# Moving the attention norm's scale per token from the operand of the query, key and value projections to their results

## The chip, the cores and the metric

The kernel runs on one core of one Trainium2 chip. The metric is the device time of one execution in microseconds (us). Three executions of the kernel before gave 984.69, 985.72 and 985.86 us.

## The reference

Two transformer blocks run one after the other on 256 tokens of width 1024, all in 32-bit floats. The change concerns the seam between them: the first block ends in a modulated norm, and the second begins with an attention norm and the query, key and value projections.

```python
def first_block(...):
    ...
    shf, scf = jnp.split(c_act @ w_ada_f + b_ada_f, 2, axis=-1)
    return modulate(rms_norm(x, normf_w), shf, scf)

def second_block(x, attn_norm, w_qkv, ...):
    h = x
    y = rms_norm_2(h, attn_norm[i])
    qkv = (y @ w_qkv[i]).reshape(B, S, 3, N_HEADS, HEAD_DIM)
    ...
    o = moba_attention(q, k, v, rel_bias)
    h = h + o.transpose(0, 2, 1, 3).reshape(B, S, D) @ w_o[i]
```

`rms_norm` divides each token by the root of its mean square (plus 1e-6) and multiplies by a weight per feature; `modulate` is h * (1 + scale) + shift with a scale and a shift per feature. With 256 tokens the attention is plain causal attention of 16 heads of width 64 with a bias by distance. Its scores are divided by 8 and go through a softmax.

## The kernel before

Activations are stored transposed: 128 features on the partitions, 256 tokens along the free dimension, eight such tiles for width 1024. `X` is the residual stream. A token's scale is then a value per column, which the kernel holds in `R`, the same in all partitions: the squares of `X` are summed over features by matmuls with a matrix of ones, and ScalarE takes logarithm and exponential of the sum (`act_ln_exp`, L1315 and L1317).

**Products.** Every large product is made of three passes in a reduced format (float32r). The operand is split into a high part `HH` and a low part `HL`, the weight into `wh` and `wl`, and the matmul engine adds wh*HH, wl*HH (L997) and wh*HL (L1003). A unit is four 128-row slices of a weight by 256 output columns; it is done as two tiles of twelve matmuls, one for each 128 outputs, and a projection product has two units, so four tiles. Value products swap the operands, so tokens lie on the partitions of their result (L995 and L1001). ScalarE rounds a unit's weight to `wh` (L1330), VectorE subtracts to get `wl` (L1682), in five buffers in turn: the split of the unit four ahead waits until the unit before the running one is done with its buffer.

**The seam.** The last product of the first feed-forward network ends in `close`: VectorE adds it to `X` (L1743), ScalarE squares, the matmul engine sums, then does two sets of nine small warming matmuls (L1112), and ScalarE makes `R`. Then `after` writes the modulated `X` in place: VectorE multiplies by weight and scale (`shift`, L1752), ScalarE adds the shift (L1384). ScalarE and VectorE square these tiles by turns (L1356, L1715), the matmul engine sums them (L1159, L1160), ScalarE makes the second `R`, and `apply` makes the operands: VectorE multiplies `X` by the attention norm's weight and `R` into `tmp` (`dve_scale`, L1644), ScalarE rounds to `HH` (L1305), VectorE and GpSimd subtract to `HL` (L1657, L1901). Only then can the first query product start. The feed-forward norm of the first block uses the same `apply` with a shift: there ScalarE makes the odd tiles in two steps (L1307, L1309) and the even ones in one (L1311).

**Attention.** Products come in the order q0, k0, q1, k1, v0, q2, k2, v1, q3, k3, v2, v3, each with 256 outputs, that is four heads. ScalarE evacuates each result from its accumulation bank (`act_evacuate`: L1234 for queries, with the factor 1/8, L1236 for keys, L1238 for values). Four heads at a time go through `attend`: scores on the matmul engine (L1094, L1095), bias and maximum on VectorE (L1567, L1569), exponentials on ScalarE (L1282, L1284), division on VectorE (L1577, L1578), transposes on the matmul engine (L1100), and the product with the values (L1106, L1107).

**What sets the order.** A planner written in Python (`run`, `after`, `tick`) puts out one list of events. Each engine walks it and takes its own part, so each engine's order is fixed when the kernel is built, and engines wait for one another on semaphores. Tasks such as `attend` are generators that `tick` advances by a step after each tile of a product.

## Time and profile before

| | us |
|---|---|
| three executions, median | 985.72 |
| the profiled execution | 986.15 |
| its span on the core | 984.4 |
| matmul engine busy | 939.0 |
| VectorE busy | 677.4 |
| ScalarE busy | 505.7 |
| GpSimd busy | 75.3 |
| DMA, mean rate | 180 GB/s |

The span is cut by time: the mixer of the first block comes first, its feed-forward network ends near 647, the seam lies from there to 663, the projections and the attention to about 758, and the second feed-forward network fills the rest. Busy times are sums over the span; what counts for the time is which engine the others wait for. A timeline lists an engine's instructions by start in microseconds from the span's start, with the idle time before one and what released it. The granted clock is TensorE's, 1.00 for its full 2.4 GHz and 0.50 for 1.2 GHz.

### The profile page before, as it was taken

The numbers are of one execution on the slowest core, as the hardware profiler recorded it, in microseconds if no ns is written. First come the engines' busy times: TensorE is split into PE (matmuls) and PEld (weight loads), VectorE is DVE, ScalarE is ACT, GpSimd is POOL, SyncE is SP. The second block draws the span as 40 slices with busy tenths as digits, with TensorE's granted clock in tenths as the row PEclk, the third lists the DMA queues.
The fourth block names the chain that finished last, engine by engine and source line by source line (L and its number), as shares of the span: only waits on it lengthen the run. The fifth ranks groups of instructions, "written<-read, shape, count | busy, mean of one in ns | idle before, by whom it ended". The sixth has DMA issues, their size and how long they took to land.

```text
span 984.4 us, 17542 instructions
## 1 busy us (share of the span) xinstructions
PE 939.0 (95%) x7500; PEld 898.9 (91%) x7500; DVE 677.4 (69%) x1102; ACT 505.7 (51%) x805; POOL 75.3 (8%) x91
## 2 busy tenths in 40 slices
PE   6789999999999999999998999989999999999997
PEld 2588998998999999999998999979998999999997
DVE  3877678567569888678677774556665677777643
ACT  2476666544343456556334443456665465666442
POOL 0101112112100000021000000110000300000001
PEclk9799999999999999999999999999999999999999
DMA  8733222222248977455899775514442354554631
GB/s 321 281 144 120 87 87 86 87 91 87 82 166 299 337 288 273 154 201 212 243 271 338 270 279 182 202 46 172 134 156 97 129 172 174 187 197 161 219 135 43
DMA packets 27677, 177.41 MB, mean 180 GB/s; under 512 B 2864, under 2 KB 5680, under 8 KB 7504
## 3 DMA queue, kind: packets, MB, share of 16 engines
q1 hardware_dynamic: 27600, 176.30, 51.2%
q8 instruction: 59, 0.97, 0.4%
q14 instruction: 18, 0.15, 0.1%
HBM read 174.45 MB, written 1.84 MB: 179 GB/s over the span
## 4 chain that ended last, share of the span: by engine, by line
PE 71%; DVE 13%; DMA 7%; ACT 7%; issue 2%; SPq 0%; DVEq 0%; ACTq 0%
PE ps L997 37%; PE ps L1003 19%; DVE wl L1682 3%; DMA raw<-in_w_fi_dram 3%; DVE acc L1617 2%; ACT wh L1330 2%; PE ps L1050 2%; PE ps L995 2%; PE ps L1039 2%; DMA raw<-in_w_sc_dram 1%; DMA raw<-in_w_rest_dram 1%; DVE tmp L1644 1%; PE ps L1046 1%; DMA raw<-in_w_in_dram 1%; PE ps L1132 1%
## 5 line engine op out<-in xcount | busy, mean ns | idle before, releaser
L997 PE MATMUL ps<-HH,wh 128*128 128x256 f32 x1480 | 386.1, 293 | 7.0 <-DVE wl L1682 6.1
L1682 DVE TENSOR_TENSOR wl<-raw,wh 128x1024 fp32r<-128x1024 f32 x265 | 321.8, 1235 | 99.5 <-ACT wh L1330 98.9
L997 PE MATMUL ps<-HH,wl 128*128 128x256 f32 x1480 | 374.4, 285 | 0.0
L1330 ACT ACTIVATE wh<-raw 128x1024 fp32r<-128x1024 f32 x265 | 272.3, 1040 | 175.5 <-PE ps L1003 105.3
L997 PEld LDWEIGHTS ps<-HH,wh 128*128 128x128 f32 x1480 | 286.2, 193 | 13.8 <-issue 8.6
L997 PEld LDWEIGHTS ps<-HH,wl 128*128 128x128 f32 x1480 | 286.3, 193 | 2.0 <-issue 2.0
L1003 PE MATMUL ps<-HL,wh 128*128 128x256 f32 x1480 | 241.2, 285 | 2.6 <-DVE HL L1657 2.2
L1003 PEld LDWEIGHTS ps<-HL,wh 128*128 128x128 f32 x1480 | 207.1, 194 | 3.4 <-DVE HL L1657 2.6
L997 PE MATMUL ps<-FH,wl 128*128 128x256 f32 x352 | 88.8, 285 | 0.0
L997 PE MATMUL ps<-FH,wh 128*128 128x256 f32 x352 | 88.1, 279 | 0.0
L1617 DVE SCALAR_TENSOR_TENSOR acc<-raw,silc,acc 128x512 f32<-128x512 f32 x101 | 76.6, 759 | 8.7 <-DMA raw<-in_ada_dram 5.7
L997 PEld LDWEIGHTS ps<-FH,wh 128*128 128x128 f32 x352 | 66.9, 190 | 0.0
L1600 DVE SCALAR_TENSOR_TENSOR tmp<-ps,vec,tmp 128x255 f32<-128x255 f32 (+2 forms) x112 | 46.1, 475 | 29.5 <-ACT tmp L1400 27.8
L997 PEld LDWEIGHTS ps<-FH,wl 128*128 128x128 f32 x352 | 66.0, 187 | 0.0
L1003 PE MATMUL ps<-FL,wh 128*128 128x256 f32 x352 | 57.8, 282 | 0.0
L1906 POOL TENSOR_TENSOR sq<-sq 128x256 f32<-128x256 f32 x12 | 10.7, 888 | 600.2 <-ACT sq L1368 600.2
L1003 PEld LDWEIGHTS ps<-FL,wh 128*128 128x128 f32 x352 | 48.9, 188 | 0.0
L1534 DVE TENSOR_TENSOR xz<-xz,ps 128x512 f32<-128x512 f32 x32 | 21.8, 687 | 32.1 <-PE ps L1050 32.1
L1491 ACT ACTIVATE FH<-tmp 128x512 fp32r<-128x512 f32 x22 | 13.9, 633 | 58.0 <-DVE tmp L1846 30.4
L997 PE MATMUL ps<-YH,wh 128*128 128x256 f32 x128 | 32.2, 281 | 1.4 <-DVE wl L1682 1.4
L997 PE MATMUL ps<-YH,wl 128*128 128x256 f32 x128 | 32.1, 284 | 0.0
L1400 ACT ACTIVATE tmp<-ps,vec 128x256 f32<-128x256 f32 x44 | 22.3, 556 | 14.7 <-PE ps L1003 14.7
(251 smaller groups left out, 1148.1 us busy)
## 6 DMA issues: line engine op xcount, KB each, us to landing
raw<-in_ada_dram SPq DMA_DIRECT2D x32, 1024.0 KB, 5.2
raw<-in_w_fi_dram SPq DMA_DIRECT2D x22, 1024.0 KB, 5.0
raw<-in_w_up_dram SPq DMA_DIRECT2D x22, 1024.0 KB, 4.8
raw<-in_w_rest_dram SPq DMA_DIRECT2D x20, 1024.0 KB, 4.9
raw<-in_w_in_dram SPq DMA_DIRECT2D x16, 1024.0 KB, 4.8
raw<-in_w_qkv_dram SPq DMA_DIRECT2D x12, 1024.0 KB, 4.8
raw<-in_w_o_dram SPq DMA_DIRECT2D x8, 1024.0 KB, 4.9
raw<-in_w_fo_dram SPq DMA_DIRECT2D x8, 1024.0 KB, 5.1
```

What stands on the lines that cost most here:

```text
L995: e.matmul(o, x_hi[:, k0 + k, 128 * t:128 * t + 128], w[:, k, :], start=first and n + k == 0, **MM)
L997: e.matmul(o, w[:, k, 128 * t:128 * t + 128], x_hi[:, k0 + k, :], start=first and n + k == 0, **MM)
L1003: ins = e.matmul(o, wh[:, k, 128 * t:128 * t + 128], x_lo[:, k0 + k, :], start=False, **MM)
L1039: ins = e.matmul(bank[:, cs[c]], S[f"d{n % 2}"][:, c, :], xz[:, 0, c, :], start=True, **MM)
L1050: ins = e.matmul(bank[:, 256 + 128 * c:384 + 128 * c], S["y"][:, c, :], xz[:, 1, c, :], start=True, **MM)
L1330: e.activation(whl[u % HALF][0][:, 0:n], raw[i % RAW][:, c:c + n], ACT.Copy).then_inc(*a_hi.up(u))
L1400: e.activation(tmps[m][:, T * t:T * t + T], b[:, T * t:T * t + T], ACT.Identity, scale=v("conv2", 88 + ft), bias=v("conv2_b", ft)).then_in ...
L1491: e.activation(flat(dst, j), tmps[m][:, :], ACT.Copy).then_inc(*a_ev.up("hi", src, j))
L1534: e.tensor_tensor(xz4, xz4, b[:, :], ALU.subtract).then_inc(*v_gdn.up("xz", h, n))
L1600: e.scalar_tensor_tensor(out=cv, in0=b[:, T * t:T * t + T - s], scalar=tap, in1=cv, op0=ALU.mult, op1=ALU.add).then_inc(*v_ev.up("conv", n ...
L1617: ins = e.scalar_tensor_tensor(out=acc_, in0=w, scalar=c, in1=acc_, op0=ALU.mult, op1=ALU.add)
L1682: e.tensor_tensor(wl[:, 0:n], raw[i % RAW][:, c:c + n], wh[:, 0:n].bitcast(F32), ALU.subtract).then_inc(*v_lo.up(u))
```

## The change

The scale of the attention norm is a factor per token, so it can be left out of the operand and multiplied into the result. The operand becomes X * w1n * R + shn, where `R` is now the scale of the first block's last norm, `w1n` its weight times the attention norm's and `shn` the modulation's shift times the attention norm's weight. `apply(N3)` makes it straight from `X` before `X` is modulated, with the instructions of the feed-forward norm. The modulation of `X`, its squares, their sums and the second scale move into a task, `third_norm`, which runs beside the first query product; its scale is kept in `R3`, an eighth of it in `R3q`, and, turned by two matmuls of one column, per partition in `r3c`. Queries and keys are evacuated by VectorE with a multiplication by `R3q` or `R3`, values by ScalarE in two halves with `r3c`. The vectors `w1c`, `w1n` and `shn` are made ahead of the closing residual. The second set of warming matmuls goes.

```diff
+    w1n = sb("w1n", [128, 8])
+    shn = sb("shn", [128, 8])
...
+    R3 = sb("R3", [128, T], where=phase)
+    R3q = sb("R3q", [128, T], where=phase)
+    r3c = sb("r3c", [128, 2], where=phase)
...
+    def third_norm():
+
+        bank, before = yield from take(misc)
+        for i in range(4):
+            emit("shift", N2, i)
+            s, sfree = yield from take(sq)
+            yield
+            emit("norm_sq", N3, i, s, sfree, bank, before if i == 0 else None)
+            sq.give(s, p_norm, "sq", N3, i)
+        yield
+        emit("norm_r", N3, bank)
+        made.add("norm_r3")
+        misc.give(bank, a_norm, "ln", N3)
+        yield
+        bank, before = yield from take(misc)
+        emit("norm_col", N3, bank, before)
+        made.add("norm_col")
+        misc.give(bank, a_norm, "col")
+        misc.order[:] = [b for b in misc.order if b[0] == 3]
...
         elif kind in ("q2", "k2", "v2"):
-            emit("plain", p["p"], 0)
-            main.give(banks[0], a_ev, "plain", p["p"])
+            until("norm_r3" if kind != "v2" else "norm_col")
+            if kind == "v2":
+                emit("plain", p["p"], 0)
+                main.give(banks[0], a_ev, "plain", p["p"])
+            else:
+                emit("normed", p["p"], 0)
+                main.give(banks[0], v_ev, "normed", p["p"])
...
+            if n == N1:
+                mod(4)
+                mod(3)
+                emit("mod_scale", n, 0)
+            elif n == N2:
+                mod(7)
+                mod(6)
+                emit("mod_scale", n, 0)
             close(n, p)
             for t in range(2):
                 main.give(banks[t], v_ev, "x", n, 6 + t)
             if n == N1:
-                mod(4)
-                mod(3)
-                emit("mod_scale", n, 0)
                 apply(n)
             elif n == N2:
-                mod(7)
-                mod(6)
-                emit("mod_scale", n, 0)
-                bank, before = misc.take()
-                for i in range(4):
-                    emit("shift", n, i)
-                    if i:
-                        s, sfree = sq.take()
-                        emit("norm_sq", N3, i - 1, s, sfree, bank, before if i == 1 else None)
-                        sq.give(s, p_norm, "sq", N3, i - 1)
-                s, sfree = sq.take()
-                emit("norm_sq", N3, 3, s, sfree, bank, None)
-                sq.give(s, p_norm, "sq", N3, 3)
-                wbank, wfree = misc.take()
-                emit("norm_r", N3, bank, wbank, wfree)
-                misc.give(wbank, p_norm, "warm", N3)
-                misc.give(bank, a_norm, "ln", N3)
                 apply(N3)
-                misc.order[:] = [b for b in misc.order if b[0] == 3]
+                tasks.append(third_norm())
...
-            a_ev.wait_ge(e, "plain", named["q2", j]["p"])
-            a_ev.wait_ge(e, "plain", named["k2", j]["p"])
+            v_ev.wait_ge(e, "normed", named["q2", j]["p"])
+            v_ev.wait_ge(e, "normed", named["k2", j]["p"])
...
-            elif kind == "norm_r" and ev[1] == N3:
-                warm(e, N3, *ev[3:])
+            elif kind == "norm_col":
+                b = ev[2]
+                free(e, ev[3])
+                a_norm.wait_ge(e, "r", N3)
+                for t in range(2):
+                    ins = e.matmul(psum[b][:, t:t + 1], R3[0:1, cs[t]], ones[0:1, 0:1], start=True, **MM)
+                ins.then_inc(*p_norm.up("col"))
...
-        elif kind == "q2":
-            ins = e.activation(flat(QA, j), bank[:, :], ACT.Copy, scale=0.125)
-        elif kind == "k2":
-            ins = e.activation(flat(KA, j), bank[:, :], ACT.Copy, scale=1.0)
         else:
-            ins = e.activation(VA[:, :, 256 * j:256 * j + 256], pair(bank), ACT.Copy)
+            a_norm.wait_ge(e, "col")
+            e.activation(VA[:, 0, 256 * j:256 * j + 256], bank[:, 0:T], ACT.Copy, scale=r3c[:, 0:1]).then_inc(
+                *a_ev.up("plain_0", n))
+            ins = e.activation(VA[:, 1, 256 * j:256 * j + 256], bank[:, T:2 * T], ACT.Copy, scale=r3c[:, 1:2])
...
+                act_ln_exp(e, n, b)
                 if n == N3:
-                    v_norm.wait_ge(e, "shift", 7)
-                act_ln_exp(e, n, b)
+                    a_norm.wait_ge(e, "r", N3)
+                    e.activation(R3q[:, :], R3[:, :], ACT.Copy, scale=0.125).then_inc(*a_norm.up("rq"))
+            elif kind == "norm_col":
+                p_norm.wait_ge(e, "col")
+                e.activation(r3c[:, :], psum[ev[2]][:, 0:2], ACT.Copy).then_inc(*a_norm.up("col"))
...
+            x_ready(e, N2 if n == N3 else n, kt)
+            w = {N3: w1n[:, kt:kt + 1], N4: v("ffn_norm", kt)}.get(n, w1c[:, kt:kt + 1])
...
+        if n == N2:
+            mod_ready(e, 12, 13)
+            e.tensor_tensor(shn[:, :], modc[:, 48:56], v("attn_norm", 0, 8), ALU.mult).then_inc(*v_norm.up("shn"))
+            v_norm.wait_ge(e, "w1c", N2, 0)
+            e.tensor_tensor(w1n[:, :], w1c[:, :], v("attn_norm", 0, 8), ALU.mult).then_inc(*v_norm.up("w1n"))
...
+            elif kind == "normed":
+                p = products[ev[1]]
+                finished(e, p)
+                a_norm.wait_ge(e, "rq" if p["kind"] == "q2" else "r", *(() if p["kind"] == "q2" else (N3,)))
+                dst, r = (QA, R3q) if p["kind"] == "q2" else (KA, R3)
+                e.tensor_tensor(dst[:, 2 * p["j"]:2 * p["j"] + 2, :], pair(psum[p["banks"][0]]),
+                                r[:, None, :].broadcast_to([128, 2, T]), ALU.mult).then_inc(
+                    *v_ev.up("normed", ev[1]))
```

The matmul engine's order at the seam before (`ps` are banks, `sq` squares, `cst` the ones and the identity, `wh0` and `wl0` the first unit's weight):

```order
L1112 MATMUL ps4<-cst 128x128 x9
L1159 MATMUL ps4<-sq2,cst 128x256
L1160 MATMUL ps4<-sq2,cst 128x256
L1159 MATMUL ps4<-sq0,cst 128x256
L1160 MATMUL ps4<-sq0,cst 128x256
L1159 MATMUL ps4<-sq1,cst 128x256
L1160 MATMUL ps4<-sq1,cst 128x256
L1159 MATMUL ps4<-sq2,cst 128x256
L1160 MATMUL ps4<-sq2,cst 128x256
L1112 MATMUL ps3<-cst 128x128 x9
L997 MATMUL ps2<-HH,wh0 128x256
```

And now, from the warming matmuls on; between the last rows of a pair and the next pair stands one tile:

```order
L1130 MATMUL ps4<-cst 128x128 x9
L1015 MATMUL ps2<-HH,wh0 128x256
...
L1021 MATMUL ps2<-HL,wh0 128x256 x4
L1177 MATMUL ps4<-sq2,cst 128x256
L1178 MATMUL ps4<-sq2,cst 128x256
L1015 MATMUL ps2<-HH,wh0 128x256
...
L1177 MATMUL ps4<-sq2,cst 128x256
L1178 MATMUL ps4<-sq2,cst 128x256
L1184 MATMUL ps3<-cst,R3 128x1 x2
L1015 MATMUL ps0<-HH,wh2 128x256
```

The four pairs of ones matmuls moved from ahead of the query product to behind each of its four tiles, and the two one-column matmuls stand between the last pair and the key product.

ScalarE's order at the seam before, from the shifts of `X` to the weight splits:

```order
L1384 ACTIVATE X<-X,modc 128x256 x4
L1356 ACTIVATE sq2<-X 128x512
L1384 ACTIVATE X<-X,modc 128x256 x4
L1356 ACTIVATE sq1<-X 128x512
L1315 ACTIVATE R<-ps4,cst 128x256
L1317 ACTIVATE R<-R 128x256
L1305 ACTIVATE HH<-tmp3 128x256 x2
L1305 ACTIVATE HH<-tmp0 128x256 x2
L1305 ACTIVATE HH<-tmp1 128x256 x2
L1305 ACTIVATE HH<-tmp2 128x256 x2
L1330 ACTIVATE wh4<-raw0 128x1024
```

And now, from the last rounding to `HH` on:

```order
L1333 ACTIVATE HH<-tmp2 128x256
L1413 ACTIVATE X<-X,modc 128x256 x2
L1355 ACTIVATE wh4<-raw0 128x1024
L1381 ACTIVATE sq2<-X 128x512
L1413 ACTIVATE X<-X,modc 128x256 x4
L1355 ACTIVATE wh0<-raw0 128x1024
L1381 ACTIVATE sq1<-X 128x512
L1413 ACTIVATE X<-X,modc 128x256 x2
L1340 ACTIVATE R3<-ps4,cst 128x256
L1342 ACTIVATE R3<-R3 128x256
L1388 ACTIVATE R3q<-R3 128x256
L1391 ACTIVATE r3c<-ps3 128x2
```

Shifts, squares and the second logarithm and exponential moved behind the roundings, with two weight splits (`wh4`, `wh0`) between them.

VectorE's order ahead of the second group of heads before (`OLl` is the output of the group before, `ISA` the bias and maximum):

```order
L1581 TENSOR_TENSOR OLl<-ps6,OHh 64x256
L1581 TENSOR_TENSOR OLl<-ps7,OHh 64x256
L1567 ISA ap0,ast0<-ps4,U 128x128
L1567 ISA ast0 128x1
L1569 ISA ap0,ast0<-ps4,U 128x256
L1569 ISA ast0 128x1
L1572 TENSOR_SCALAR ast0<-ast0 128x2
```

And now:

```order
L1610 TENSOR_TENSOR OLl<-ps6,OHh 64x256
L1610 TENSOR_TENSOR OLl<-ps7,OHh 64x256
L1838 TENSOR_TENSOR QA<-ps1,R3q 128x512
L1596 ISA ap0,ast0<-ps4,U 128x128
L1596 ISA ast0 128x1
L1598 ISA ap0,ast0<-ps4,U 128x256
L1598 ISA ast0 128x1
L1601 TENSOR_SCALAR ast0<-ast0 128x2
```

The evacuation of the query product moved from ScalarE to this place, ahead of the first head's bias and maximum; the third group of heads has the same rows.

## Rows read from the trace of the kernel before

**Rows 1.** The page, the chain that ended last, share of the span by engine.
```profile
PE 71%; DVE 13%; DMA 7%; ACT 7%; issue 2%; SPq 0%; DVEq 0%; ACTq 0%
```

**Rows 2.** Waits of the matmul engine, 640 to 790: us in all, times, longest.
```profile
PE ps L1100 <- DVE ap L1578: 2.1, 6, 0.4
```

**Rows 3.** Timeline of VectorE around the norm: start us, us, instructions [idle before <-releaser].
```profile
645.93 0.48 DVE L1743 SCALAR_TENSOR_TENSOR X<-ps,modc,X 128x256 f32<-128x256 f32 x1 [1.22 <-PE ps L1003]
...
647.05 0.16 DVE L1667 SCALAR_TENSOR_TENSOR w1c<-modc,vec 128x8 f32<-128x8 f32 x1
649.33 2.46 DVE L1752 SCALAR_TENSOR_TENSOR X<-X,w1c,R 128x256 f32<-128x256 f32 x6 [2.12 <-ACT R L1317]
...
658.59 1.67 DVE L1644 SCALAR_TENSOR_TENSOR tmp<-X,vec,R 128x256 f32<-128x256 f32 x4 [4.03 <-ACT R L1317]
```

**Rows 4.** The same of ScalarE.
```profile
649.85 1.71 ACT L1384 ACTIVATE X<-X,modc 128x256 f32<-128x256 f32 x4 [0.55 <-DVE X L1752]
651.47 0.61 ACT L1356 ACTIVATE sq<-X 128x512 f32<-128x512 f32 x1
```

**Rows 5.** The same of the matmul engine.
```profile
652.22 0.67 PE L1159 MATMUL ps<-sq,cst 128*128 128x256 f32 x2 [1.88 <-ACT sq L1356]
...
654.13 1.06 PE L1160 MATMUL ps<-sq,cst 128*128 128x256 f32 x2
654.98 1.06 PE L1159 MATMUL ps<-sq,cst 128*128 128x256 f32 x2
...
657.44 2.17 PE L1112 MATMUL ps<-cst 128*128 128x128 f32 x18
...
663.08 0.28 PE L997 MATMUL ps<-HH,wh 128*128 128x256 f32 x1
...
667.38 0.28 PE L997 MATMUL ps<-HH,wh 128*128 128x256 f32 x1
```

**Rows 6.** Timeline, feed-forward norm: VectorE twice, ScalarE, matmul engine.
```profile
444.61 1.68 DVE L1644 SCALAR_TENSOR_TENSOR tmp<-X,w1c,R 128x256 f32<-128x256 f32 x4 [2.14 <-ACT R L1317]
...
450.85 0.48 DVE L1614 TENSOR_SCALAR acc<-raw,silc 128x512 f32<-128x512 f32 x1
...
451.04 1.99 ACT L1330 ACTIVATE wh<-raw 128x1024 fp32r<-128x1024 f32 x2
...
449.26 0.27 PE L997 MATMUL ps<-HH,wh 128*128 128x256 f32 x1
```

**Rows 7.** Stretches: us, busy (instructions) by engine, granted clock, DMA share, GB/s.
```profile
653.10:656.30 3.20, 3.20 (x10) 2.45 (x9) 0.78 (x2) 1.16 (x3) 0.00 (x0) 0.50 0.02 5
...
752.50:755.30 2.80, 1.64 (x9) 0.93 (x9) 2.32 (x11) 2.80 (x11) 0.00 (x0) 1.00 0.81 334
755.50:758.50 3.00, 3.00 (x16) 2.19 (x18) 1.26 (x2) 2.17 (x7) 0.00 (x0) 0.50 0.01 3
```

**Rows 8.** Timeline of VectorE, first group of heads.
```profile
675.01 0.29 DVE L1567 CUSTOM_DVE_ANT_0 ap<-ps,U 128x128 f32<-128x128 f32 x1 [2.23 <-PE ps L1095]
...
679.54 0.35 DVE L1578 TENSOR_SCALAR ap<-ap,ast 128x256 f32<-128x256 f32 x1
...
681.51 0.35 DVE L1578 TENSOR_SCALAR ap<-ap,ast 128x256 f32<-128x256 f32 x1
```

**Rows 9.** Timeline, second group of heads: VectorE, ScalarE, matmul engine twice.
```profile
701.38 0.29 DVE L1567 CUSTOM_DVE_ANT_0 ap<-ps,U 128x128 f32<-128x128 f32 x1 [2.35 <-PE ps L1095]
...
703.77 0.60 ACT L1234 ACTIVATE QA<-ps 128x512 f32<-128x512 f32 x1 [3.62 <-PE ps L1003]
...
707.89 1.44 PE L1100 MATMUL ps<-cst,ap 128*128 128x128 f32 x9
709.67 0.55 PE L1100 MATMUL ps<-cst,ap 128*128 128x128 f32 x3 [0.33 <-DVE ap L1578]
```

**Rows 10.** Groups by shape: busy us, mean ns | idle before <-releasers.
```profile
L1846 DVE TENSOR_TENSOR tmp<-tmp,ps 128x512 f32<-128x512 f32 x11 | 7.5, 685 | 6.3 <-PE ps L1003 6.3
...
L1406 ACT ACTIVATE tmp<-ps,vec 128x256 f32<-128x256 f32 x8 | 3.4, 470 | 8.1 <-PE ps L1003 8.1
```

More of the change, by code:

```diff
@@ L1300, in act_parts @@
                 finished(e, named[before_write[n]])
-            shift = {N0: modc[:, kt:kt + 1], N1: modc[:, 24 + kt:25 + kt]}.get(n)
+            shift = {N0: modc[:, kt:kt + 1], N1: modc[:, 24 + kt:25 + kt], N3: shn[:, kt:kt + 1]}.get(n)
+            if n == N3:
+                v_norm.wait_ge(e, "shn")
             if n in (N0, N1):
@@ L1313, in act_ln_exp @@
     def act_ln_exp(e, n, b):
+        r = R3 if n == N3 else R
         ln_exp(e)
-        e.activation(R[:, :], psum[b][:, 0:T], ACT.Ln, scale=1.0 / 1024, bias=eps).then_inc(*a_norm.up("ln", n))
+        e.activation(r[:, :], psum[b][:, 0:T], ACT.Ln, scale=1.0 / 1024, bias=eps).then_inc(*a_norm.up("ln", n))
         a_norm.wait_ge(e, "ln", n)
-        e.activation(R[:, :], R[:, :], ACT.Exp, scale=-0.5).then_inc(*a_norm.up("r", n))
+        e.activation(r[:, :], r[:, :], ACT.Exp, scale=-0.5).then_inc(*a_norm.up("r", n))
     def scalar_engine(e):
@@ L1636, in dve_scale @@
     def dve_scale(e, n, j, m, before):
-        a_norm.wait_ge(e, "r", n)
+        a_norm.wait_ge(e, "r", N2 if n == N3 else n)
         if n in (N0, N1):
             v_norm.wait_ge(e, "w1c", n, j // 2 if n == N0 else 0)
+        if n == N3:
+            v_norm.wait_ge(e, "w1n")
         free(e, before)
         for kt in (2 * j, 2 * j + 1):
-            x_ready(e, n, kt)
-            w = {N3: "attn_norm", N4: "ffn_norm"}.get(n)
-            e.scalar_tensor_tensor(out=tmps[m][:, T * (kt % 2):T * (kt % 2) + T], in0=X[:, kt, :],
-                                   scalar=w1c[:, kt:kt + 1] if w is None else v(w, kt), in1=R[:, :], op0=ALU.mult,
-                                   op1=ALU.mult).then_inc(*v_norm.up("scaled", n, kt))
+            x_ready(e, N2 if n == N3 else n, kt)
+            w = {N3: w1n[:, kt:kt + 1], N4: v("ffn_norm", kt)}.get(n, w1c[:, kt:kt + 1])
+            e.scalar_tensor_tensor(out=tmps[m][:, T * (kt % 2):T * (kt % 2) + T], in0=X[:, kt, :], scalar=w,
+                                   in1=R[:, :], op0=ALU.mult, op1=ALU.mult).then_inc(*v_norm.up("scaled", n, kt))
     def dve_parts(e, n, j, m):
@@ L1651, in dve_parts @@
         src, high = tmps[m][:, 0:T], HH[:, kt, :].bitcast(F32)
-        if n in (N0, N1):
-            shift = modc[:, kt:kt + 1] if n == N0 else modc[:, 24 + kt:25 + kt]
+        if n in (N0, N1, N3):
+            shift = {N0: modc[:, kt:kt + 1], N1: modc[:, 24 + kt:25 + kt], N3: shn[:, kt:kt + 1]}[n]
             ins = e.scalar_tensor_tensor(out=HL[:, kt, :], in0=src, scalar=shift, in1=high, op0=ALU.add,
```

## The prediction

> **What bounds the kernel now.** I read the page first. The chain that ended last lies on the matmul engine for 71% of the span [rows 1], so a step pays where it takes a wait away from that engine, and costs where it puts one there. Next come the matmul engine's waits in the stretch that the change rebuilds: the attention transposes wait 2.1 us in six pieces [rows 2]. The timelines of three engines then show the norm itself. VectorE gets the scale of the first block's last norm at 649.33 [rows 3]. ScalarE's shift of a tile follows VectorE's by 0.52 us, four shifts take 1.71 us and a 128x512 square 0.61 us [rows 4]. The matmul engine waits 1.88 us for the first squares, starts the sums at 652.22 and ends them at 657.44; 1.15 us later VectorE has the second scale [rows 3, 5]. It reaches tile 2 of the query product (a tile is twelve matmuls, four per product) at 663.08 and the key product at 667.38, so three tiles take 4.30 us, 1.43 each [rows 5]. That is the stage to beat: from 649.33 to 667.38, 18.05 us.
>
> Inside it the clock matters. After 1.88 us without work the sums run at half: the granted clock is 0.50 from 653.1 to 656.3 (the lower level, 1.2 GHz, where 1.00 is 2.4 GHz) [rows 7]; I put its return at 656.5, 4.3 us after work resumed at 652.22 [rows 5]. At the lower level a ones matmul takes 0.85 us (654.13 to 654.98) [rows 5], at the full one half of that, so a pair costs 1.70 or 0.85.
>
> **The change, part by part.** Times t count from 649.33, when VectorE has the first scale in either kernel.
>
> *Operands without the second norm.* Scaling, shifting and splitting has a model in the feed-forward norm, which has the same instructions and starts at 444.61: tile 1 ends there at 449.26, VectorE is free at 450.85, ScalarE at 451.04 [rows 6]. So tile 1 ends at t = 4.65, VectorE is free at 6.24, ScalarE at 6.43. Before, tile 1 ended at t = 13.75. The matmul engine is 9.1 us ahead here.
>
> *The norm beside the product.* In the new order a pair of ones matmuls stands behind each of the four tiles. Each engine works in order, so tile 2 can't start before the first squares. VectorE starts the first two tiles of the residual stream at 6.24 and 6.64 (six took 2.46 us [rows 3]); ScalarE shifts them from 6.76 to 7.6, then has a weight split to do (1.99 us for two [rows 6], so 0.95), and squares at 8.55 to 9.16. The pair starts 0.14 later, at 9.3: **4.65 us idle**, more than twice the idle time that was followed by the half clock. I therefore take the lower level from 9.3 on, and 4.3 us of it, as before: pair 1 to 11.0, tile 2 to 13.7. ScalarE's next split waits for tile 2 (its buffer), 13.8 to 14.8; it squares to 15.4, shifts the last two tiles to 16.15, and VectorE squares them to 16.9. The matmul engine meanwhile: pair 2 to 14.6 (0.85 again), tile 3 to 16.0, pair 3 to 16.9, tile 4 to 18.3, pair 4 to 19.2. Logarithm and exponential with their hand-overs take the 1.15 us seen at 657.44, to 20.35, and the two one-column matmuls, which wait for them, about 0.4: the key product starts at t = 20.75 where it did at 18.05. **+2.7 us.** At the full level all along the same steps give pair 1 to 10.15, tile 2 to 11.6, squares and pair 4 to 17.1, the key product at 18.6: +0.55. These are the ends of the range for this term. I take the first, since an idle stretch less than half as long was enough.
>
> *Key evacuation on VectorE.* The nearest row is a 128x512 multiply out of PSUM, 685 ns [rows 10], against 0.60 us on ScalarE [rows 9]: +0.1 us ahead of the first scores. The weight split now behind it delays VectorE by as little.
>
> *Query evacuation ahead of the scores.* For query products 2 and 3 VectorE's order is now: evacuate the query product, then add bias and find the maxima of four heads. The product is only finished one tile behind those heads' score matmuls. Before, ScalarE evacuated it at 703.77, while VectorE had begun on the scores at 701.38 and their last transposes started at 709.67, 0.33 us after the ones before [rows 9]. Now VectorE waits until 703.77, evacuates for 0.61 (685 ns less the 0.08 by which neighbours overlap) and begins on the scores at 704.38. From there to the last normalized tile the first group of heads needs 6.85 us (675.01 to 681.51 + 0.35) [rows 8]: 711.23. The last transposes follow at once, **1.6 us** later than the 709.67 of before, and the matmul engine has nothing else, since the next tile stands behind them. ScalarE saves its 0.6 us of evacuation, but no longer sets the pace. Bounds: nothing, if ScalarE still did, to 3.0 us, the whole delay at the start. The working lies between and I keep it: twice, **+3.2 us**. Later splits slip by 3 us and are made three products' units ahead, so they cover it.
>
> *Value evacuation in two.* Two scaled copies (470 ns each [rows 10], the second some 0.05 earlier than end to end) take 0.87 instead of 0.60 us. Three of the four stand ahead of no exponentials; the last heads the chain of waits to the last heads' exponentials: **+0.25 us**.
>
> *Small ones.* The scale vectors made ahead of the closing residuals: one takes 0.16 us, and at the attention norm VectorE was idle 1.22 us ahead of them, which hides all three [rows 3]; at the feed-forward norm I grant no such cover, +0.1 us. The copy of the scale for queries costs ScalarE 0.4 us while the key product runs: nothing. The nine warming matmuls that go were inside a wait.
>
> Sum: 2.7 + 0.1 + 3.2 + 0.25 + 0.1 = 6.35 us on the profiled execution's 986.15. That run is 0.43 above the median of 985.72; on the median I say **992.1 us**.
>
> **A rule against a row.** From 752.5 to 755.3 the matmul engine was busy 1.64 of 2.80 us at the full clock, with no wait over 0.4 us, and yet the clock was at half from 755.5 to 758.5 [rows 2, 7]. The new stalls in the two middle groups of heads look alike: twelve transposes spread over 3.7 us, first gap 1.3 us (they began at 707.89 [rows 9]; the heads' last steps on VectorE come 0.66 us apart [rows 8] and end at 711.23, so the first tile is there at 709.25). The Trainium skill, TensorE: Matmul & The Clock Gate, section "Why this matters for your kernels", blames idle gaps between bursts of matmuls, and asks that none be long. By that rule the transposes would keep the full clock and the sum stands; by the row it may fall there too, which is rival 1. The trace agrees with the rule at 653 and goes beyond it at 755.
>
> **The rivals.**
> 1. *The clock falls in the middle groups too.* For: the row just named. Against: in those groups before, transposes with single gaps of 0.33 us did not bring it. A stretch of 3.0 to 3.2 us at the half level [rows 7] costs up to 1.6 us where the engine has work: 993.7 with one, 995.3 with both.
> 2. *The clock holds beside the first product.* Then 2.7 becomes 0.55: 989.9. Against it stands the stretch at 653.1 [rows 7].
> 3. *The norm is hidden after all* (the other side). If each square is ready when its pair is reached, the matmul engine goes through: 4.65 + four pairs 3.5 + three tiles 4.3 + 1.5 for the scale = t 13.95, which is 4.1 us earlier than before. With the other terms, 3.65, the time is 985.3, not slower. It decides at the first pair: the squares would have to be ready by t = 4.65, while VectorE is bound to splitting operands until 6.24. If only the later pairs are in time, the 4.65 us of idle time stand and nothing is won.
> 4. *The stalls in the middle groups are absorbed*: the working gives a wait of 1.6 us, its lower bound none. Without them 988.9.
>
> **How the numbers follow.** Forecast 0.42; rival 1 0.30 (two groups, each about one in five); rival 2 0.13; rival 4 0.08; rival 3 0.05; something else 0.02. The range takes the forecast, rivals 1 and 2: low 989.0 is just under rival 2, high 995.6 just above rival 1 with both groups. A measurement of this kernel can tell about 0.2%, 2.0 us, from no change. Slower by more than that (over 987.7) are all cases but rival 3 and part of the rest: 0.93. Rival 3 lies within 0.2%: 0.04 of it there, and 0.03 for faster in all, where the clock also happens to hold where it fell before.
>
> **What the new profile would show.** The first tile of the query product ends near t = 4.65, then the matmul engine waits some 4.6 us for a square of ScalarE, at half clock afterwards; the key product starts 20 to 21 us behind the first scale. A wait of about 1 us stands ahead of the one-column matmuls. In the two middle groups VectorE idles until the query product's last matmul, and transposes wait for VectorE some 1.3 us at first. Wrong would be: a wait under 2 us ahead of the first pair, a key product earlier than t = 18, or transposes that still end ScalarE's chain.

## The result and the profile after

| | median us | executions | ratio to the kernel before | 95% interval |
|---|---|---|---|---|
| kernel before | 985.3 | 20 | | |
| changed kernel | 989.6 | 20 | 1.0045 | 1.0032 to 1.0059 |

The change costs 4.4 us (3.2 to 5.8, the ratio's interval times 985.3). The forecast was 992.1, with 989.0 to 995.6 as its range.

The profiled execution of the changed kernel took 984.37 us, the lowest of its twenty, so its end says nothing; distances inside it do. The stage begins again where VectorE has the first scale, here at 642.78 (t = 0), where [rows 3] has 649.33. First the chain that ended last and the matmul engine's waits, 640 to 790:

```profile
PE 80%; DVE 10%; ACT 5%; DMA 3%; issue 1%; SPq 0%; DVEq 0%; ACTq 0%
```

```profile
PE ps L1177 <- ACT sq L1381: 4.9, 1, 4.9
PE ps L1118 <- DVE ap L1607: 4.3, 6, 1.2
...
PE ps L1184 <- ACT R L1342: 1.0, 1, 1.0
```

The 1.9 us ahead of the first ones matmuls [rows 5] have become 4.9, and the transposes' 2.1 [rows 2] have become 4.3; a wait of 1.0 for the scale is new. The timelines of the matmul engine, VectorE and ScalarE at the seam show how:

```profile
652.53 1.19 PE L1177 MATMUL ps<-sq,cst 128*128 128x256 f32 x2 [4.94 <-ACT sq L1381]
...
663.63 0.60 PE L1184 MATMUL ps<-cst,R 1*128 1x1 f32 x4 [1.01 <-ACT R L1342]
671.05 0.50 PE L1112 MATMUL ps<-KA,QA 64*128 64x128 f32 x4 [0.87 <-DVE KA L1838]
```

```profile
642.78 1.67 DVE L1675 SCALAR_TENSOR_TENSOR tmp<-X,w1n,R 128x256 f32<-128x256 f32 x4 [2.19 <-ACT R L1342]
...
649.02 1.36 DVE L1787 SCALAR_TENSOR_TENSOR X<-X,w1c,R 128x256 f32<-128x256 f32 x2
```

```profile
650.41 0.51 ACT L1413 ACTIVATE X<-X,modc 128x256 f32<-128x256 f32 x1 [0.38 <-DVE X L1787]
...
651.77 0.61 ACT L1381 ACTIVATE sq<-X 128x512 f32<-128x512 f32 x1
```

VectorE starts the residual stream at t = 6.24, as forecast; ScalarE shifts two tiles, splits a weight and squares at 8.99; the first sums start at 9.75 (forecast 9.3). The first scores start at t = 28.27, where they started at 24.75 before. And in this execution the granted clock falls inside the wait already, at t = 7.48, and is back at t = 14.31 (the columns of [rows 7]):

```profile
647.00:650.00 3.00, 0.51 (x2) 0.30 (x2) 3.00 (x7) 2.06 (x5) 1.42 (x2) 1.00 0.00 0
650.00:652.00 2.00, 0.00 (x0) 0.00 (x0) 2.00 (x4) 1.62 (x4) 0.10 (x1) 0.56 0.00 0
652.00:655.00 3.00, 2.47 (x7) 2.14 (x8) 1.99 (x5) 1.75 (x5) 0.00 (x0) 0.50 0.77 257
...
657.00:660.00 3.00, 3.00 (x22) 2.81 (x21) 0.31 (x1) 2.38 (x4) 0.00 (x0) 0.99 0.00 0
```

In the second group of heads, VectorE first, then the matmul engine and its clock:

```profile
700.76 0.69 DVE L1838 TENSOR_TENSOR QA<-ps,R3q 128x512 f32<-128x512 f32 x1 [4.49 <-PE ps L1021]
...
707.86 0.35 DVE L1607 TENSOR_SCALAR ap<-ap,ast 128x256 f32<-128x256 f32 x1
```

```profile
706.29 2.88 PE L1118 MATMUL ps<-cst,ap 128*128 128x128 f32 x12 [1.25 <-DVE ap L1607]
```

```profile
707.00:709.00 2.00, 1.78 (x10) 1.30 (x11) 1.96 (x6) 1.35 (x3) 0.00 (x0) 0.82 0.81 336
709.00:712.00 3.00, 3.00 (x17) 3.00 (x17) 0.58 (x2) 0.67 (x2) 0.00 (x0) 0.55 0.21 87
```

VectorE stands idle for 4.49 us, from 696.27 on. The matmul engine makes the scores of the four heads from 697.42 to 699.10, but VectorE waits for the query product, evacuates it, and only then begins on the scores, at 701.37. The last division ends 6.84 us after that (forecast 6.85). Behind these transposes the clock is at half: rival 1, in one of the two groups.

One thing did not fit. Ahead of t = 0 the two kernels do nearly the same (the change only adds some small vectors), and yet the changed one gets there 6.6 us earlier. The second part of the experiments is about that.

### The profile page after: what moved, and what is told of

It is laid out like the page before. It is cut to its first block, busy times and chain, and to the rows that moved or that the text cites. A ratio compares the mean times of both kernels' runs of the same rounds, so it can differ in the third digit from the quotient of the medians.

```text
span 982.6 us, 17538 instructions
## 1 busy us (share of the span) xinstructions
PE 930.7 (95%) x7486; PEld 892.0 (91%) x7486; DVE 681.1 (69%) x1112; ACT 506.7 (52%) x807; POOL 74.7 (8%) x91
## 4 chain that ended last, share of the span: by engine, by line
PE 80%; DVE 10%; ACT 5%; DMA 3%; issue 1%; SPq 0%; DVEq 0%; ACTq 0%
PE ps L1015 43%; PE ps L1021 21%; DVE wl L1717 2%; DMA raw<-in_w_fi_dram 2%; PE ps L1013 2%; PE ps L1068 2%; PE ps L1057 2%; DVE tmp L1675 1%; ACT wh L1355 1%; PE ps L1064 1%; PE ps L1150 1%; PE ps L1019 1%; DMA raw<-in_ada_dram 1%; PE ps L1167 1%; DMA raw<-in_w_rest_dram 1%
```

## The experiments on the two stalls

The edits of this section are made to the changed kernel. Ratios are to the kernel before, run in turn on the same chip. In the profiles I read distances from the first scale (t = 0).

**Warming matmuls in the first wait.**

```diff
+            if i == 0:
+                wbank, wfree = yield from take(misc)
+                emit("warm_seam", 0, 0, wbank, wfree)
+                misc.give(wbank, p_norm, "warm", N3)
...
+                for _ in range(9):
+                    e.matmul(psum[ev[3]][:, 0:128], ones, eye, start=True, **MM)
+                warm(e, N3, ev[3], None)
```

> The changed kernel with eighteen warming matmuls (128x128, into a bank that nobody reads) ahead of the first pair of ones matmuls, where the matmul engine waits 4.9 us for ScalarE's square. In the changed kernel the key product starts 21.4 us behind the stage's first scale and the time is 989.6 us, 1.0045 of the kernel before. Theory A (the seam costs its idle time and, on top, the half clock that follows it): granted clock 1.00 behind the wait, a ones matmul 0.43 us instead of 0.85, tile 2 in 1.4 instead of 2.9 us, key product at 19.0 to 19.6 us, time 987.6 (ratio about 1.0025). Theory B (the half clock costs nothing here, because squares and splits of the other engines end as late as before): key product still at 21 to 21.5 us, time 989.6 (ratio 1.0045). Theory C (an idle wait filled with warming matmuls does not hold the clock): as B in time, with granted clock 0.50 behind the wait.

986.25 us, ratio 1.0002 (0.9984 to 1.0020). Timeline of the matmul engine, then two stretches of it:

```profile
653.16 3.49 PE L1186 MATMUL ps<-cst 128*128 128x128 f32 x18
656.49 2.17 PE L1134 MATMUL ps<-cst 128*128 128x128 f32 x18
658.50 0.60 PE L1181 MATMUL ps<-sq,cst 128*128 128x256 f32 x2
```

```profile
652.50:656.00 3.50, 3.43 (x16) 3.43 (x17) 3.50 (x8) 2.18 (x6) 1.52 (x2) 0.51 0.00 0
656.00:660.00 4.00, 4.00 (x34) 3.90 (x34) 2.98 (x6) 2.75 (x6) 0.00 (x0) 1.00 0.52 147
```

The clock fell here too, at 652.50 in the last matmuls of tile 1, but the warming matmuls took most of it, and it was back before the sums. These start 0.5 us later (t = 10.24, the warming overran), and still the one-column matmuls come at t = 19.24 instead of 20.85, the key product at 19.74 instead of 21.38 (A said 19.0 to 19.6), and the first scores at 26.62 instead of 28.27. Theory A holds: the half level costs at least 1.6 us here. In time the edit gave back 4.2 us (the ratios' difference), more than A said; the section on the clock comes back to it.

**The queries and keys evacuated by ScalarE.** This leaves out the per-token factor on queries and keys.

```diff
-                emit("normed", p["p"], 0)
-                main.give(banks[0], v_ev, "normed", p["p"])
+                emit("plain", p["p"], 0)
+                main.give(banks[0], a_ev, "plain", p["p"])
```

> The changed kernel with the query and key products evacuated by ScalarE with a plain copy, as in the kernel before; this leaves out the per-token factor on queries and keys. Everything else of the change stays, the seam too. Theory A (a query evacuation on VectorE ahead of the scores costs 1.6 us in each of two middle groups of heads, the key's 0.1): time from the finished query product 2 to the finished value product 3 shorter by 3.2 us, time 986.3 (ratio about 1.001), and VectorE's wait of 4.5 us for the matmul engine ahead of the query evacuation gone. Theory B (the seam is all, the middle groups absorb their delay): 989.6 (ratio 1.0045). Theory C (A, and the clock falls in those groups too, which this takes away): up to 4.8 us shorter, 984.8.

**The query evacuation behind the scores, on VectorE.**

```diff
+    def late(p):
+        while ("att", 4 * p["j"] - 1 - 4, 1) not in made:
+            yield
+        emit("normed", p["p"], 0)
+        main.give(p["banks"][0], v_ev, "normed", p["p"])
...
+            elif kind == "q2" and j > 1:
+                tasks.append(late(p))
```

> The changed kernel with query products 2 and 3 evacuated on VectorE still, times the per-token scale, but behind the scores of the previous group's fourth head instead of ahead of its first. Nothing is left out. Theory A (it is the place in VectorE's order that costs 1.6 us a group, not the engine): as with ScalarE's evacuation, 986.3 to 986.5 (ratio about 1.001); VectorE no longer waits 4.5 us ahead of the evacuation. Theory B (the 0.69 us that VectorE spends on it is what costs, wherever it stands): no change, or at most 1 us less than 989.6. Theory C (the bank held longer stalls the value or next key product): a new wait of the matmul engine for the query evacuation, and 989.6 or more.

On ScalarE: 984.4 us, ratio 0.9989 (0.9971 to 1.0007). Late on VectorE: 983.9 us, 0.9985 (0.9963 to 1.0006). Start of the scores of the third and fourth group, in the changed kernel (the second group's is at 697.42) and in the late version:

```profile
723.45 0.50 PE L1112 MATMUL ps<-KA,QA 64*128 64x128 f32 x4
747.96 0.50 PE L1112 MATMUL ps<-KA,QA 64*128 64x128 f32 x4
```

```profile
723.51 0.50 PE L1120 MATMUL ps<-KA,QA 64*128 64x128 f32 x4
746.00 0.50 PE L1120 MATMUL ps<-KA,QA 64*128 64x128 f32 x4
```

A group takes 24.51 us in the changed kernel at full clock (26.03 in the group where it fell), 22.90 before and with ScalarE's evacuation, 22.49 here. So the evacuation ahead of the scores costs 24.51 - 22.90 = **1.61 us** a group, the 1.6 of the sum, and theory A holds: it is its place in the order, not the engine and not its 0.69 us. Behind the scores it even gains 0.4. No new wait came in its place (theory C there), and the transposes wait 2.2 us in all, 2.1 before [rows 2]. Both versions come out about 2 us under A's time, near the 984.8 of the first one's theory C, by which the clock no longer falls in these groups; in neither profile it did.

**The sums further back.** The pairs of ones matmuls stand behind tiles 3 and 4 of the query product and 1 and 2 of the key product, squares ahead of weight splits on ScalarE, and queries and keys 0 are evacuated when the scale is there.

```diff
+        slots = []
+        for i in range(3):
             emit("shift", N2, i)
...
+            emit("norm_sq", N3, i, s, sfree, bank, None)
...
+        for i in (1, 2, 3):
+            yield
+            emit("norm_mm", N3, i, slots[i], bank, None)
+            sq.give(slots[i], p_norm, "sq", N3, i)
...
+                begin(evacuate(p))
```

> The changed kernel with the pairs of ones matmuls moved back: behind tiles 3 and 4 of the query product and tiles 1 and 2 of the key product instead of behind tiles 1 to 4, the one-column matmuls behind tile 3 of the key product, squares issued ahead of weight splits on ScalarE; query and key product 0 are evacuated once the scale is there. Nothing is left out. Theory A (the change loses because the sums stand too early in the matmul engine's order, not because the idea is wrong): the wait for the first square shrinks from 4.9 to 1 to 2 us, and the first scores start 20.8 us (full clock) to 22.7 us (half clock behind that wait) behind the stage's first scale, against 28.3 in the changed kernel and 24.75 in the kernel before. Time 5.6 to 7.5 us under the changed kernel: 982 to 984 (ratio 0.9965 to 0.9985), with the middle groups' stalls still in it. Theory B (VectorE or ScalarE bounds the seam: splits, squares, residual stream): the first scores start at 25 us or later, and the time is 986 or more.

981.9 us, ratio 0.9973 (0.9955 to 0.9990). Timeline of the matmul engine:

```profile
655.97 0.67 PE L1196 MATMUL ps<-sq,cst 128*128 128x256 f32 x2 [1.27 <-ACT sq L1400]
...
668.67 0.50 PE L1130 MATMUL ps<-KA,QA 64*128 64x128 f32 x4 [0.88 <-DVE KA L1857]
```

The wait for the first square is 1.27 us, the one for the scale is gone, the clock stays at 1.00, and the first scores start 21.75 us behind the first scale at 646.92: 3.0 earlier than in the profile of before, and 1.7 earlier than in the two later profiles of the kernel before (further down), in which the clock did not fall here. Theory A holds. What the seam lost, it lost by the place of the sums in the matmul engine's order, not by the idea of moving them.

**Both**, the edit above with the late evacuation:

```diff
+    def late(p):
+        while ("att", 4 * p["j"] - 1 - 4, 1) not in made:
+            yield
+        yield from evacuate(p)
...
+            elif kind == "q2" and j > 1:
+                tasks.append(late(p))
```

> The moved sums and the late evacuations together; nothing is left out. Theory A (the two costs are separate and add up): first scores 21 to 22 us behind the first scale, as with the moved sums alone, and 22.5 us from group to group, as with the late evacuations alone; against the moved sums alone 4 us less: 978 (ratio about 0.993). Theory B (what is won in the groups is lost again at a later wait, as the weight splits that VectorE makes ahead get later): 22.9 us or more from group to group, or a new wait of the matmul engine for a split; 980 to 982.

**976.95 us, ratio 0.9921 (0.9906 to 0.9936)**: faster than both kernels. The first scores start at t = 21.76, the groups take 22.48 us each: the two gains add up. Not all of the 7.8 us under the kernel before is the change's own: the run with padding below shows that 3.6 of it can be had without the change.

## The experiments on what did not fit

**Both kernels once more.**

> The kernel before, unchanged, profiled once more on the chip that ran the experiments. In the profile shown ahead of the prediction the last first-block norm's first scale stood at 649.33, in the changed kernel's at 642.78, in its four variants at 645.8 to 648.3, although the code ahead of it is nearly the same. Theory A (executions differ, the kernels don't: the number of stretches at the lower clock and the pace of the matmuls): first scale at 643 to 648 here too, and every difference from the changed kernel accounted for by such stretches. Theory B (the scale vectors made ahead of the closing residuals, which the prediction priced at +0.1, or another part of the change, gain 3 us ahead of the stage): 648 to 650 again. Behind that scale both expect the anchors of the first profile: first scores 24.75 us later, 22.9 us from group to group.

> The changed kernel, unchanged, profiled once more. Its first profile is of one of its fastest executions (984.4 where the median is 989.6), with 27 us in all at the lower clock; the other executions' mean clock of 0.98 says some 40 us. Theory A: a profile nearer the median shows the same anchors (first pair 9.7 us behind the first scale, 24.5 us from group to group at full clock) and more stretches at the lower clock, each worth 1.5 to 1.7 us: behind the wait at the seam up to 10 us of it instead of 6.9, and one in a middle group. Theory B (something else varies): the same stretches and another time.

The changed kernel again gave 990.0 us, ratio 1.0056 (1.0041 to 1.0072). Both new profiles show the lower clock in the same places ahead of t = 0, and for equally long. Timeline of VectorE, kernel before, then changed kernel:

```profile
648.49 0.88 DVE L1752 SCALAR_TENSOR_TENSOR X<-X,w1c,R 128x256 f32<-128x256 f32 x2 [2.12 <-ACT R L1317]
```

```profile
646.48 0.88 DVE L1675 SCALAR_TENSOR_TENSOR tmp<-X,w1n,R 128x256 f32<-128x256 f32 x2 [2.20 <-ACT R L1342]
```

The two executions of the kernel before reach this point 0.84 us apart, the two of the changed kernel 3.70: so 4.5 of the 6.6 us go between executions of one kernel, as in theory A. 2.0 remain at equal clock, so neither theory holds as it stood. Behind the first scale the new profile of before does not repeat the old one either: its first scores start at t = 23.47 and not at the 24.75 that both theories expected, because the clock did not fall at the seam. The place is the pace of one kind of matmul. First and last row of the second network's down product, which nothing interrupts, in the kernel before and in the changed one (first profiles; the second ones give the same distances):

```profile
912.09 0.28 PE L997 MATMUL ps<-FH,wh 128*128 128x256 f32 x1
...
975.21 0.40 PE L1003 MATMUL ps<-FL,wh 128*128 128x256 f32 x2
```

```profile
911.73 0.28 PE L1015 MATMUL ps<-FH,wh 128*128 128x256 f32 x1
...
973.45 0.39 PE L1021 MATMUL ps<-FL,wh 128*128 128x256 f32 x2
```

63.12 us against 61.72, for the same 528 matmuls at the same full clock: 120.0 ns from start to start, and 117.3. On `HH` and `HL` both kernels run at 120. What differs is where `FH` lies in memory: the change declares 64 bytes per partition (`w1n`, `shn`) behind `HH` and ahead of `FH`, `YH` and `OHh`.

**Only the place, in the kernel before.**

```diff
+    pad = sb("pad", [128, 16])
     adr = sb("adr", [128, 4])
```

> The kernel before with 64 bytes per partition of unused memory where the changed kernel declares its two new vectors; not one instruction differs. In the profiles the start-to-start time of the 128x256 matmuls at full clock differs by operand: on FH and FL (1056 of them) 120.0 ns in the kernel before, 117.1 to 117.4 in the changed one, on YH and YL (384) 119.5 to 120.1 against 117.3 to 118, on OHh and OLl (192) 120 against 112.9 to 117.3, but on HH and HL, which lie ahead of the new vectors, 120 in both. FH and YH lie 96 bytes past a multiple of 128 before, 32 past it in the changed kernel, HH at a multiple in both. Theory A (the place of the operand in memory sets the pace): 117 to 117.5 ns on FH, YH and OHh here too, and 1632 x 2.8 ns = 4.6 us less, bounds 3 to 5: 980.3 (ratio 0.995 to 0.997). Theory B (something else in the changed kernel, or chance): 120 ns on all of them and 985 (ratio 1.000).

980.9 us, ratio 0.9963 (0.9945 to 0.9980), with not one instruction changed. The down product again:

```profile
910.07 0.28 PE L998 MATMUL ps<-FH,wh 128*128 128x256 f32 x1
...
971.79 0.39 PE L1004 MATMUL ps<-FL,wh 128*128 128x256 f32 x2
```

61.72 us. Theory A holds, as far as this run goes.

It also sets the scale for the versions above. The sums moved back alone (0.9973) are no faster than this kernel (0.9963), and both moves together (0.9921) are faster by 0.0042, or 4.1 us, about 1.9 to 6.4 with both intervals. So the improved change does gain something of its own, but about half of what its ratio to the kernel before suggests.

**The change without the place.**

```diff
-    w1n = sb("w1n", [128, 8])
-    shn = sb("shn", [128, 8])
...
-    R3 = sb("R3", [128, T], where=phase)
...
                   st=sb(f"ast{i}", [128, 8], where=phase), bank=psum[4 + i]) for i in range(4)]
+    R3 = sb("R3", [128, T], where=phase)
...
+    w1n = sb("w1n", [128, 8], where=phase)
+    shn = sb("shn", [128, 8], where=phase)
```

> The changed kernel with its five new tiles moved behind the attention heads' own, so that every other tile lies where it does in the kernel before; not one instruction differs from the changed kernel. Theory A (the operands' place gave the change a gain that the prediction did not see): 120 ns on FH, YH and OHh, and 1056 x 2.8 + 384 x 2 + 192 x 2.8 to 7 ns = 4.3 to 5 us more than the changed kernel: 994 to 995 (ratio 1.009 to 1.010); the change itself then costs 8.5 to 9.5 us. Theory B (no such effect): 989.6 (ratio 1.0045).

992.35 us, ratio 1.0069 (1.0047 to 1.0091), and the down product takes 63.12 us again (918.45 to 981.57). The pace is A's. The time is under its 994: 2.4 us above the first ratio of the changed kernel, and the two intervals overlap, so the size rests on the padded kernel before rather than on this run.

**All operands at another place.** Padding in the version with both moves (for 32 bytes `pad0` has 8 columns):

```diff
+    pad0 = sb("pad0", [128, 16])
     HH = sb("HH", [128, 8, T], F32R)
...
+    pad1 = sb("pad1", [128, 24])
     mixer = ExitStack()
...
+    pad2 = sb("pad2", [128, 24], where=phase)
     QA = sb("QA", [128, 8, T], where=phase)
```

> The version with the sums moved and the late evacuations (976.95 us), with unused memory of 64 and 96 bytes per partition in three places, so that HH, HL, YH, YL, FH, FL, OHh and OLl all begin 64 bytes past a multiple of 128; no instruction differs. Theory A (the pace depends on that place; 64 bytes past gave 112.9 to 117.3 ns on OHh): HH's and HL's 4440 matmuls gain 2.8 to 7 ns each, 12 to 31 us: 945 to 965 (ratio 0.96 to 0.98). Theory B (the place relative to the weight tiles or another thing decides, not the place itself): 975 to 979.

> As the aligned version (969.5 us; its operands 64 bytes past a multiple of 128), with all eight moving operands 32 bytes past it. If 32 is as good as 64: 117.3 ns on HH, HL, FH and OHh, and 968 to 972 (ratio 0.983 to 0.987). If 64 has an advantage of its own (113 to 115 ns were seen there on OHh, and on HH in one stretch): no mean under 117 anywhere, and 970 to 974.

969.5 us, ratio 0.9850 (0.9825 to 0.9874), with 64 bytes; 969.8, 0.9861 (0.9838 to 0.9884), with 32. The second network's first product, all on `HH` and `HL`, from its first row to its last, without padding, with 64 and with 32 bytes:

```profile
774.98 0.36 PE L1040 MATMUL ps<-HH,wh 128*128 128x256 f32 x1
...
903.17 0.64 PE L1046 MATMUL ps<-HL,wh 128*128 128x256 f32 x4
```

```profile
768.01 0.36 PE L1043 MATMUL ps<-HH,wh 128*128 128x256 f32 x1
...
893.90 0.63 PE L1049 MATMUL ps<-HL,wh 128*128 128x256 f32 x4
```

```profile
770.34 0.36 PE L1043 MATMUL ps<-HH,wh 128*128 128x256 f32 x1
...
895.08 0.63 PE L1049 MATMUL ps<-HL,wh 128*128 128x256 f32 x4
```

128.19, 125.89 and 124.74 us. At 120.0 ns a matmul, the 1052 from the first row to the last make 126.2 of the 128.19 us; the other 1.95 us are the same in all three, so the paces are 117.8 ns with 64 bytes and 116.8 with 32. The gain is there, but smaller than A's 12 to 31 us for 64 bytes: 969.5 us where A said 945 to 965. The faster pace does occur with 64 bytes, over whole products, such as the mixer's output product on `YH` in the same profile:

```profile
390.93 0.28 PE L1043 MATMUL ps<-YH,wh 128*128 128x256 f32 x1
...
412.24 0.62 PE L1049 MATMUL ps<-YL,wh 128*128 128x256 f32 x4
```

These are 21.31 us for 188 matmuls, 113.4 ns each, where the changed kernel (32 bytes) has 117.3 and the kernel before 120.0. With 32 bytes no product ran below 116.7, and the time is the same. The matmul engine also catches up with the weight splits: it waits 9.9 us for them over the span instead of 7.7:

```profile
PE ps L1040 <- DVE wl L1743: 7.7, 4, 4.1
```

```profile
PE ps L1043 <- DVE wl L1746: 9.9, 4, 5.8
```

**Everything moved together.** The version with both moves:

```diff
+    pad = sb("pad", [128, 16])
     raw = [sb(f"raw{i}", [128, 2048]) for i in range(RAW)]
```

> The version with the sums moved and the late evacuations, with 64 bytes of unused memory ahead of the very first tile, so that every tile in it moves by 64 bytes together and none moves against another: the weight tiles and HH now begin 64 bytes past a multiple of 128 (before 0), FH and YH 96 (before 32), OHh 0 (before 64). Theory A (the operand's own place past a multiple of 128 decides: 0 and 96 gave 120 ns, 32 and 64 gave 113 to 117.5): 117.5 ns on HH and HL, 120 on FH, YH and OHh; 4440 x 2.5 less, 1632 x 2.8 more: 6 to 8 us under 976.95, 969 to 971 (ratio 0.984 to 0.986). Theory B (the place relative to the weight tiles decides): 120 on HH, 117.3 on FH as without the pad, 977 (ratio 0.992).

978.0 us, ratio 0.9937 (0.9915 to 0.9958): theory B. The first product takes 128.19 us again, although `HH` lies where it gave 125.89, and the down product the short 61.72, although `FH` lies where it gave 63.12 in the kernel before:

```profile
775.56 0.35 PE L1041 MATMUL ps<-HH,wh 128*128 128x256 f32 x1
...
903.75 0.64 PE L1047 MATMUL ps<-HL,wh 128*128 128x256 f32 x4
```

```profile
904.23 0.28 PE L1041 MATMUL ps<-FH,wh 128*128 128x256 f32 x1
...
965.95 0.39 PE L1047 MATMUL ps<-FL,wh 128*128 128x256 f32 x2
```

So it is not the operand's own place that counts but its distance, modulo 128 bytes, from tiles declared ahead of it, all of which moved along here. I take the weight tile, which is the other tile that these matmuls read; no run moves it alone, so that it is this tile, and not the tiles of raw weights or of `X` beside it, is not shown. By that distance, 0 and 96 gave about 119 to 122 ns on every operand. 32 gave 116.5 to 118 on `HH`, `FH` and `YH` and 119 on the small `OHh` product. 64 gave 117.8 on `FH`, 113 to 118 on `HH` and `YH`, and 114.7 or 118.8 on the last 168 matmuls of `OHh`, the two values in two executions of the same changed kernel. So the distance alone does not set the faster pace. Why it counts is open, and so is whether 113 can be had at will.

## The clock over all executions

Over its twenty executions the changed kernel's mean granted clock is 0.9797, over 35 of the kernel before it is 0.9845. Inside the twenty, time and clock go together (from 984.4 us at 0.985 to 992.9 at 0.977): a straight line through them gives 0.88 us for 0.001. By that slope the difference of 0.0048 is worth 4.2 us, about the whole of the 4.4. With warming matmuls the mean was 0.9857, with both moves 0.9868. So most of the loss goes with the lower level. That is a correlation and an upper bound, since the part of it that lies inside a wait costs nothing. It is not the whole story either: the two versions with the query evacuation moved have 0.981, worth 1.1 us by the same slope, and are 5.5 and 5.9 us faster than the changed kernel. The plain idle time, 3.2 us in the two groups and what the seam loses at full clock, was largely paid for by the faster matmuls.

Where it falls is partly chance, partly the kernel's doing. At the seam it fell in all five profiles with the wait of 4.9 us and nothing in it, for 6.8 to 10.2 us. With the kernel before's wait of 1.9 it fell in one profile of three. With the sums moved back, where the wait is 1.3, it fell in one of five, and in that one ahead of the wait, from t = 4.10 on. The stretches of that profile (everything moved together, first scale at 646.75):

```profile
646.80:650.80 4.00, 3.08 (x19) 2.20 (x17) 4.00 (x8) 3.44 (x9) 1.50 (x2) 1.00 0.01 4
650.80:654.20 3.40, 3.15 (x14) 3.15 (x15) 3.40 (x7) 2.27 (x5) 1.52 (x2) 0.51 0.00 0
```

Here the matmul engine is in tile 1, which waits for its operands in pieces of 0.2 to 0.4 us, none longer. With the warming matmuls it fell at t = 4.24, and in two of the five profiles with the long wait at t = 4.57 and 4.78, where tile 1 ends at 4.8. So the long wait is not all that brings the fall: tile 1 is enough in some executions. What the runs show is that it fell in two of six profiles where the wait was short or filled, and in five of five where it was long and empty. In the two middle groups it fell once in four of five profiles with the query evacuation ahead of the scores, and in none of the nine others.

## Why the prediction was right, and where its sizes were off

- *Direction and range.* Right: slower, inside the range, 2.5 us under the forecast. The two stalls that the forecast rests on, the sums at the seam and the evacuation ahead of the scores, are there, and each goes away when its place in the order is changed.
- *"That is the stage to beat: ... 18.05 us."* This baseline came from an execution in which the clock had fallen. The two later profiles of the kernel before, padded or not, kept it and had the first scores at t = 23.47 instead of 24.75. In such executions the seam's loss is larger.
- *Seam, +2.7.* Mechanism right: tile 1 in time, the wait of 4.65 measured as 4.94, half the clock behind it. Size too small: the first scores come 3.5 us later than in the same profile of before (0.1 of it is the key evacuation), and 4.8 later than in those that kept the clock. Against those the baseline is the larger part of the error, 1.3 of 2.0. The path itself was 0.6 us short: the sums start at 9.75 (forecast 9.3) and the key product at 21.38 (20.75). "4.3 us of it", counted from the sums, came out in this profile, with 4.6 (9.75 to 14.31), but not its reason: the clock fell ahead of the sums, and in other profiles the lower level lasted 10.2 us. That costs less than it looks, since much of it lies inside the wait: with 10.2 us, from t = 4.57, the changed kernel's second profile has the first scores only 0.24 us later.
- *Key evacuation, +0.1.* The wait ahead of the first scores went from 0.78 to 0.87 us.
- *Query evacuation, +1.6 twice.* Measured 1.61 at full clock. Rival 4 fell.
- *Rival 1 (0.30).* It happened in four of the five profiles with the evacuation ahead of the scores, each time in one of the groups; that group took 26.03 instead of 24.51 us, so 1.5. It should have been the forecast. *The rule against the row:* the row was the better guide. Here the longest gap in such a group was 1.25 us, and the clock fell behind it. The Trainium skill, TensorE: Matmul & The Clock Gate, section "Why this matters for your kernels", warns of idle gaps between bursts; the gaps that it names are longer than this one, and longer than the 1.88 us at 652 too, so there also the trace goes beyond the rule, where the prediction calls the two in agreement.
- *Rival 2 and rival 3* fell: the half level and the 4.9 us wait were there in every profile. But the run with the sums moved back shows that rival 3's condition, squares ready when their pairs are reached, can nearly be made (1.27 us of wait are left), and is worth 6.5 us at the seam (28.27 to 21.75).
- *Value evacuation, +0.25.* From the start of the last value evacuation to the next norm's sums: 28.64 us in the second profile of before, 28.87 with the change and the old places: 0.23, from one profile each.
- *What the sum left out.* The change moved the operands in memory. That gives 1.40 us in each down product alone, and 3.6 us in all (2.0 to 5.4, the padded kernel before). Without it the change costs 6.8 us (4.6 to 9.0), beside the sum's 6.35. The sum's 6.35 lies there, but not because each term was exact: by the profiles the terms measure 3.4 to 4.7 for the seam, 0.1, 3.2, 0.2, and 1.5 for the fall in a group, 8.4 to 9.7 together, at the upper end of that interval. The run that gave 6.8 also had the better clock, 0.9827 on average over its six executions where the changed kernel's twenty have 0.9797; by the slope above that is worth 2.6 us. The terms left out, a gain of 3.6 and a loss of 1.5, and the low seam term partly cancelled, which brought the forecast within 2.5 us. That the time fell inside the range is in this part luck.

## What to carry to other kernels

Work that is moved beside a product must not be waited for at once: place its matmuls in an in-order engine where their inputs are ready, here two tiles later, and put an evacuation behind work that is already waiting, not ahead of it. Price a wait of the matmul engine with the clock behind it, and fill what is left of the wait. Compare layouts as well as instruction orders: a small new tile ahead of large ones changed this kernel's time by 0.4%, and a version that has such a tile is best compared with the old kernel padded in the same way.

## What was not expected of the hardware

A float32r matmul of 128x256 at full clock takes 120.0 ns from start to start or 117.3 (113 at best), by the distance of its moving operand, modulo 128 bytes, from tiles ahead of it in memory, probably its weight tile; 224 bytes per partition of unused memory are worth some 0.6% of this kernel (ratios 0.9921 and 0.9861). And of the 8.5 us between the fastest and the slowest execution of the changed kernel most goes with the lower clock: it falls at the same few places of the program, but not at all of them in every execution.
